# The first two projection steps in two halves of 256 tokens, with their weights and row tiles split over three engines

## The reference, cut to what matters

```python
x = x + layer(...)                     # SEQ 512 tokens, D_MODEL 1024, one layer
h = x * rsqrt(mean(x*x, -1) + 1e-6) * norm_g
proj = einsum('bsd,dc->bsc', h, w_in)  # 1024 -> 6656 columns
# dilated attention and block attention on parts of proj, gates, two branch
# projections, sigmoid merge, output projection, residual, final RMSNorm
```

## Time and profile before

| | |
|---|---|
| median of 3 runs | 429.91 us (429.64 to 429.94) |
| profiled execution, its own time | 429.92 us |
| its span, first to last instruction | 428.1 us |
| around the span | 1.8 us |
| PE busy | 417.7 us (98% of the span) |
| DVE, ACT, POOL busy | 302.8, 232.0, 220.9 us |
| mean granted PE clock | 0.996 |

### The profile page before, as it was taken

How to read it: one execution, slowest core, us unless ns; L and a number is a source line. 1 busy time by engine, 2 the same in 40 slices (tenths; PEclk the granted TensorE clock), 3 DMA queues, 4 the chain that set the end, 5 groups by cost and what they waited for, 6 DMA issues and landing times.

```text
span 428.1 us, 7122 instructions
## 1 busy us (share of the span) xinstructions
PE 417.7 (98%) x2526; PEld 372.5 (87%) x2526; DVE 302.8 (71%) x520; ACT 232.0 (54%) x487; POOL 220.9 (52%) x158
## 2 busy tenths in 40 slices
PE   7899999999999999999999999999999999999994
PEld 6789998889889988998888888889999999988884
DVE  3879946385856777657865773696686768589956
ACT  5745557554864764657656563454454545532634
POOL 5954533252655634574459655444335433734790
PEclk9999999999999999999999999999999999999998
DMA  8893454937899768222421335540443134199905
GB/s 272 250 262 102 152 163 143 280 132 260 278 303 388 290 213 273 100 100 54 144 99 50 100 127 205 196 136 14 122 138 108 48 116 136 38 410 393 418 7 198
DMA packets 49187, 77.23 MB, mean 180 GB/s; under 512 B 4440, under 2 KB 39296, under 8 KB 47616
## 3 DMA queue, kind: packets, MB, share of 16 engines
q1 hardware_dynamic: 44256, 67.91, 47.9%
q10 hardware_dynamic: 4896, 8.86, 5.7%
HBM read 55.73 MB, written 14.74 MB: 165 GB/s over the span
## 4 chain that ended last, share of the span: by engine, by line
PE 94%; DMA 2%; ACT 1%; DVE 1%; issue 1%; SPq 0%; DVEq 0%; ACTq 0%
PE ps L1183 15%; PE ps L1187 15%; PE ps L1184 15%; PE ps L1408 5%; PE ps L1407 5%; PE ps L1406 5%; PE ps L1224 4%; PE ps L1226 4%; PE ps L1225 4%; PE ps L1296 4%; PE ps L1277 3%; PE ps L1455 3%; PE ps L1453 3%; PE ps L1454 3%; PE ps L1315 2%; PE ps L1337 2%
## 5 line engine op out<-in xcount | busy, mean ns | idle before, releaser
L993 POOL TENSOR_TENSOR w_lo<-raw,w_hi 128x1024 fp32r<-128x1024 f32 x39 | 96.8, 2483 | 103.5 <-ACT w_hi L1507 103.5
L1183 PE MATMUL ps<-hT_hi,w_hi 128*128 128x512 f32 x240 | 95.7, 399 | 1.1 <-DVE hT_lo L1913 1.1
L1187 PE MATMUL ps<-hT_lo,w_hi 128*128 128x512 f32 x240 | 93.8, 391 | 0.0
L1184 PE MATMUL ps<-hT_hi,w_lo 128*128 128x512 f32 x240 | 93.6, 390 | 0.0
L1075 POOL TENSOR_TENSOR w_lo<-raw,w_hi 128x512 fp32r<-128x512 f32 (+1 forms) x34 | 42.5, 1270 | 49.5 <-ACT w_hi L1529 49.5
L1187 PEld LDWEIGHTS ps<-hT_lo,w_hi 128*128 128x128 f32 x240 | 45.0, 188 | 9.9
L1183 PEld LDWEIGHTS ps<-hT_hi,w_hi 128*128 128x128 f32 x240 | 45.1, 188 | 8.4 <-issue 1.3
L1184 PEld LDWEIGHTS ps<-hT_hi,w_lo 128*128 128x128 f32 x240 | 45.2, 188 | 7.0
L1224 PE MATMUL ps<-w_hi,hT_hi 128*128 128x256 f32 x160 | 45.2, 283 | 0.0
L1226 PE MATMUL ps<-w_lo,hT_hi 128*128 128x256 f32 x160 | 44.7, 279 | 0.0
L1225 PE MATMUL ps<-w_hi,hT_lo 128*128 128x256 f32 x160 | 44.6, 279 | 0.0
(11 more groups left out here) (279 smaller groups left out, 1048.0 us busy)
## 6 DMA issues: line engine op xcount, KB each, us to landing
raw<-in_w_in SPq DMA_DIRECT2D x25, 1024.0 KB, 5.6
KTs<-KTs SPq DMA_DIRECT2D x20, 256.0 KB, 4.4
folds<-folded_early SPq DMA_DIRECT2D x4, 1024.0 KB, 9.3
wq_raw<-in_w_out SPq DMA_DIRECT2D x4, 1024.0 KB, 9.7
folded<-folds SPq DMA_DIRECT2D x4, 1024.0 KB, 6.4
t_three<-output_weight_sums SPq DMA_DIRECT2D x2, 2048.0 KB, 11.5
output_weight_sums<-ws_parts ACTq DMA_DIRECT2D x6, 512.0 KB, 6.1
raw<-in_w_out SPq DMA_DIRECT2D x3, 1024.0 KB, 5.0
```

The lines of the kernel that those rows point to most:

```text
L993: nc.gpsimd.tensor_tensor(ring(w_lo, n, kt), src, ring(w_hi, n, kt).bitcast(F32), ALU.subtract).then_inc(lo_ready, 1)
L1183: pe.matmul(out, wh, hh, start=(k == 0), stop=False)
L1184: pe.matmul(out, wl, hh, start=False, stop=False)
L1187: return pe.matmul(out, wh, hl, start=False, stop=(k == kts - 1))
```

## The change

It cuts the opening into two halves of 256 tokens (row tiles 0 and 1, then 2 and 3).

- SP issues tiles 0 and 1, then the first chunk in two halves by k (k 0 to 3, k 4 to 7; all 256 columns each), then tiles 2 and 3.
- PE turns tiles 0 and 1, then runs matmuls of 256 tokens for steps 0 and 1 side by side, k by k, lows one k behind the highs. Just ahead of k = 7 it turns tiles 2 and 3 (`turn_rows`). Then follow k = 7, the last lows, and the second 256 tokens, step 0 and then step 1.
- Every tile is scaled half by ACT (high half, `scale_high_half`) and half by DVE (low half). Tile 0 is squared on ACT alone; of tiles 1, 2 and 3 ACT squares the low and DVE the high half (`square_high_half`), and `variance` adds two sums.
- The first chunk's cast and lows are made in four pieces of two k-tiles and all 256 columns: POOL does it all but the cast of piece 2, which ACT makes (`first_weights`). `lows(1)` is gone.
- The turned halves lie in banks 2 to 7 (first) and in banks 2, 3, 6, 7 (second), two k-tiles to a bank where needed. The gains are turned into bank 1, `gb_ready` comes in two steps.
- `d_hex` is made at step 10 (`spread_apart`).

The diff, cut to its core:

```diff
+PAIR_BANKS = [[2, 3, 4, 5, 6, 7, 4, 5], [2, 3, 6, 7, 2, 3, 6, 7]]
+TURN_ORDER = [[0, 1, 2, 3, 6, 7, 4, 5], list(range(8))]
+HI_TURNS = [[1, 2, 5, 6, 7, 8, 5, 6], [5, 6, 7, 8, 5, 6, 7, 8]]
+HIGH_SCALED = [1, 2, 4, 5]
 # SP
+            for i in range(2):
+                load_rows(i)
+            for e in range(2):
+                ks = slice(4 * e, 4 * e + 4)
+                sp.dma_start(first[:, ks, :], w_in_t[:, ks, at:at + 256]).then_inc(first_half_in[e], 16)
+            for i in range(2, TT):
+                load_rows(i)
 # POOL
+            for m in range(FIRST_PIECES - 1):
+                pool.wait_ge(first_half_in[m // 2], 16)
+                if m == ACT_PIECE:
+                    pool.wait_ge(opened_by_act, 3)
+                else:
+                    nc.gpsimd.tensor_copy(hi, part).then_inc(first_hi, 1)
+                    pool.wait_ge(first_hi, m + 1)
+                nc.gpsimd.tensor_tensor(lo, part, hi.bitcast(F32), ALU.subtract).then_inc(first_lo, 1)
...
 # PE
+            for i in range(2):
+                turn_rows(i)
+            for k in range(KT_D):
+                if k == KT_D - 1:
+                    for i in range(2, TT):
+                        turn_rows(i)
+                for n in range(2):
+                    first_high(n, 0, k)
+                if k:
+                    first_lows(k - 1)
+            first_lows(KT_D - 1)
+            for n in range(2):
+                for k in range(KT_D):
+                    first_high(n, 1, k)
+                    first_low_weights(n, 1, k)
+                    if k:
+                        first_low_rows(n, 1, k - 1)
+                first_low_rows(n, 1, KT_D - 1)
 # ACT
+            square_rows(0, D)
+            root(0)
+            square_rows(1, D // 2)
+            scale_high_half(0)
+            root(1)
+            scale_high_half(1)
+            turned_high(0, range(2))
+            first_weights()
+            turned_high(0, range(2, 4))
+            square_rows(2, D // 2)
+            turned_high(0, range(4, 6))
+            square_rows(3, D // 2)
+            root(2)
+            turned_high(0, range(6, KT_D))
+            scale_high_half(2)
+            root(3)
+            scale_high_half(3)
+            turned_high(1, range(KT_D))
 # DVE
+            variance(0)
+            square_high_half(1)
+            scale_low_half(0)
+            variance(1)
+            turn_gain()
+            scale_low_half(1)
+            turned_low(0, range(2))
+            halve_bias()
+            square_high_half(2)
+            turned_low(0, range(2, 4))
+            square_high_half(3)
+            variance(2)
+            turned_low(0, range(4, 6))
+            variance(3)
+            scale_low_half(2)
+            turned_low(0, range(6, KT_D))
+            scale_low_half(3)
+            turned_low(1, range(KT_D))
```

More of the change, by code:

```diff
@@ L1155, in _ @@
                 pe.matmul(ps[:, 0, 0:P], ident[:, :], ident[:, :], start=True, stop=True)
[L1157 to L1161, removed]
-                for k in range(KT_D):
[L1163 to L1172, removed]
+            pe.wait_ge(vec_in, 32)
@@ new lines, in _, with turn_rows @@
+            pe.transpose(ps[:, 1, 0:24], vecs[:, :], ident[0:24, 0:24]).then_inc(vecs_turned, 1)
+            def turn_rows(i):
+                order = TURN_ORDER[i // 2]
+                for k in order:
+                    if k == order[0]:
+                        pe.wait_ge(x_scaled, i + 1)
+                    if k == order[4]:
+                        pe.wait_ge(opened_by_act, HIGH_SCALED[i])
+                    if i == 2 and k in (0, 2):
+                        pe.wait_ge(hT_lo_ready, 6 if k else 2)
+                    last = pe.transpose(pair_place(i // 2, k)[:, P * (i % 2):P * (i % 2) + P],
+                                        xs[:, i, P * k:P * k + P], ident[:, :])
+                    if i % 2:
+                        last.then_inc(x_turned, 1)
@@ new lines, in first_high @@
+            def first_high(n, p, k):
+                if n == 0:
+                    pe.wait_ge(hT_hi_ready, KT_D * p + k + 1)
+                    if p == 0 and k // 2 == ACT_PIECE:
+                        pe.wait_ge(opened_by_act, 3)
+                    elif p == 0 and k < 6:
+                        pe.wait_ge(first_hi, k // 2 + 1)
+                    elif p == 0:
+                        pe.wait_ge(hi_ready, 2)
+                elif p == 0 and k == 0:
+                    pe.wait_ge(gb_ready, 1)
+                pe.matmul(ps[:, n, 256 * p:256 * p + 256], ring(w_hi, n, KT_D)[:, k, :], pair_of(hT_hi, p, k),
+                          start=(p == 0 and k == 0), stop=False)
@@ new lines, in first_low_weights, with first_low_rows @@
+            def first_low_weights(n, p, k):
+                if n == 0 and p == 0 and k < 6:
+                    pe.wait_ge(first_lo, k // 2 + 1)
+                elif n == 0 and p == 0:
+                    pe.wait_ge(lo_ready, 2)
+                pe.matmul(ps[:, n, 256 * p:256 * p + 256], ring(w_lo, n, KT_D)[:, k, :], pair_of(hT_hi, p, k),
+                          start=False, stop=False)
+            def first_low_rows(n, p, k):
+                if n == 0:
+                    pe.wait_ge(hT_lo_ready, KT_D * p + k + 1)
+                last = pe.matmul(ps[:, n, 256 * p:256 * p + 256], ring(w_hi, n, KT_D)[:, k, :],
+                                 pair_of(hT_lo, p, k), start=False, stop=(p == 1 and k == KT_D - 1))
+                if p == 1 and k == KT_D - 1:
+                    last.then_inc(projected, 1)
@@ L1204, in column_tile @@
                 def column_tile(k):
[L1205 to L1210, removed]
                     last = term(ps[:, pbank(n), :], k, KT_D, ring(w_hi, n, KT_D)[:, k, :],
-                                ring(w_lo, n, KT_D)[:, k, :], hT_hi[:, k, :], hT_lo[:, k, :],
-                                hh_count=k + 1 if n == 0 else 0)
+                                ring(w_lo, n, KT_D)[:, k, :], hT_hi[:, k, :], hT_lo[:, k, :])
                     if k == KT_D - 1:
@@ L1340, in values @@
                 last.then_inc(valued, 1)
-            for s in range(NS):
+            for s in range(2, NS):
                 score, turn = [], []
@@ L1607, in root, with scale_high_half @@
                 nc.scalar.activation(rstd[:, i:i + 1], rvar[:, i:i + 1], ACT.Sqrt).then_inc(rstd_ready, 1)
-            def scale_low_half(i):
+            def scale_high_half(i):
                 act.wait_ge(rstd_ready, i + 1)
[L1611 to L1617, removed]
+                half = xs[:, i, D // 2:D]
+                nc.scalar.activation(half, half, ACT.Copy, scale=rstd[:, i:i + 1]).then_inc(opened_by_act, 1)
@@ new lines, in variance, with turned_low @@
+                nc.vector.reciprocal(rvar[:, i:i + 1], var[:, i:i + 1]).then_inc(var_ready, 1)
+            def turned_low(p, ks):
+                for k in ks:
+                    dve.wait_ge(hT_hi_ready, KT_D * p + k + 1)
+                    nc.vector.scalar_tensor_tensor(out=pair_of(hT_lo, p, k), in0=pair_place(p, k),
+                                                   scalar=gb[:, k:k + 1], in1=pair_of(hT_hi, p, k).bitcast(F32),
+                                                   op0=ALU.mult, op1=ALU.subtract).then_inc(hT_lo_ready, 1)
@@ L1886, in turn_vectors, with turn_gain, halve_bias @@
+            def turn_gain():
                 dve.wait_ge(vecs_turned, 1)
-                link(nc.vector.tensor_copy(gb[:], ps[:, 7, SEQ - 24:SEQ]))
+                nc.vector.tensor_copy(gb[:], ps[:, 1, 0:24]).then_inc(gb_ready, 1)
+            def halve_bias():
+                dve.wait_ge(gb_ready, 1)
                 nc.vector.tensor_scalar(hbias[:], gb[:, 8:24], 0.5, None, ALU.mult).then_inc(gb_ready, 1)
-            for i in range(HALVED):
-                variance(i)
-                scale_rows(i, 0)
@@ L1893, in _ @@
[L1893 to L1913, removed]
-                                               in1=hT_hi[:, k, :].bitcast(F32), op0=ALU.mult,
-                                               op1=ALU.subtract).then_inc(hT_lo_ready, 1)
+            variance(0)
```

134 lines of the change are left out of this document (73 added, 61 removed).

## The result

| | before | after |
|---|---|---|
| median (17 runs each) | 429.76 us (429.42 to 430.86) | 430.37 us (430.15 to 431.8) |
| profiled execution, its own time; span | 429.92; 428.1 us | 430.72; 428.9 us |
| step 2 begins | 25.17 | 25.93 |

The ratio of the times is 1.0016 [1.0009, 1.0023]. The change costs 0.6 us: the ratio is inside the 0.2% that counts here as no change, though its interval lies above 1 and reaches 0.23%. The forecast was 431.4 (429.2 to 432.2).

The account below looks back on a forecast made before the run. PE, busy from 14.20 us, passes the opening on whole. Tile 3 scaled at 18.69 plus 7.93 puts step 2 at 26.62 against 25.17; 429.92 + 1.45 = 431.4 us, range 429.2 to 432.2.

Parts of the forecast that it names:

- Bound and passing on: PE is busy throughout from 14.20 us, so any change in the opening passes on whole; step 2 1.45 us later.
- What PE has left at S: After tile 3 is scaled (S), PE needs 7.93 us to step 2: a wait, eight transposes and 58 matmuls.
- The price of the cut: Steps 0 and 1 as 96 narrow instead of 48 wide matmuls: 11.52 against 10.97, 0.55 us.
- The port: In the opening, DVE and POOL block each other for whole instructions at SBUF; by this rule the time is 431.4 us.
- The sign that I had asked for: DVE's squares and variances of tiles 2 and 3 last 1 us and more, each ending as a POOL instruction ends.
- rival 1: No port waits in the opening, DVE's own list decides: step 2 at 24.57, 429.3 us, or 428.9 with earlier loads; 20%.
- Rival 2: Small DVE instructions, the variance sums, pass the port: 431.1 us, or 430.3 in a second form; 20%, half each.
- second form: Tile 2 lands before 11.1, its square precedes lows 1, variance 2 runs at once: S 17.57, 430.3 us; half of 20%.
- the sum's clock on POOL: Instruction-by-instruction times of POOL and DVE in the opening: lows 1 at 11.1, lows 3 until 16.77, tile 3 scaled at 18.69.
- They hardly meet before the change: Before the change POOL has no weights until 11.29; DVE's last SBUF-only opening instruction ends at 11.71, so they hardly meet.
- Loads: Chunk halves land at about 8.1 and 9.7, tiles 2 and 3 at 11.3 and 12.9, each 3.2 us later.
- rivals 3 and 4: Step 2's weights late, up to 431.9 us, 8%; PE clock falls between 14 and 18.7, 432.6 to 438 us, 7%.

Follow-up runs that it names:

- e2: The changed kernel with tiles 2 and 3 squared whole on ACT and root(3) ahead of both high halves; 429.23 us, ratio 0.9985 to the kernel before.
- e5: The kernel before, with only the matmuls of steps 0 and 1 cut into two of 256 tokens; step 2 at 25.54 us, no whole time given.
- e3: The changed kernel with POOL's four subtractions for the first chunk's lows replaced by memsets of zero, which read nothing; 428.71 us.
- f5: The changed kernel with POOL making the lows of piece 2 twice; 430.14 us.
- i2: The changed kernel itself, with no edit, profiled once more; 430.17 us.
- i1: The changed kernel with POOL's lows of piece 1 held until DVE has squared its half of tile 2; 430.74 us.
- e1: The changed kernel with the two-input sum of variance written as a tensor_scalar taking the second sum as a scalar operand; 429.96 us.
- g1: The kernel before, with only the three d_hex instructions moved to step 10; 429.17 us.
- f3: The changed kernel with only POOL's last lows of the first chunk held until tile 3 is scaled; 430.49 us.
- e4: The changed kernel with tiles 2 and 3 loaded ahead of the first chunk's second half; 431.61 us.

## Why the prediction was right or wrong

**Bound and passing on: right.** Step 2 came 0.76 later and the span grew by 0.8.

**What PE has left at S: right.** 7.94 in seven executions (e2's too), forecast 7.93. The price of the cut, 0.61 by e5, was given as 0.55.

**The port: right in mechanism and place.** Squares of 1.79 and 0.85, a last cast of 1.07, variances that wait, each ending with or shortly behind an instruction of the other engine. The sign that I had asked for, all four on DVE with 1 us and more, held for one of them only (1.79; the others 0.85, 0.44 and 0.54), but the sum itself had waits of 1.0, 0.36, 0.49 and 0.31 on them, so that sign was set too high. e3 puts its price at 1.94 us from A to S. This is also the answer to where the gain went: without these waits the same order gives 428.71, that is rival 1's 428.9 to 429.3 and a little better. The Trainium skill, SBUF — State Buffer, Who interferes with whom, says that whoever issues first gets the shared pair for the whole instruction. The trace agrees where the starts are 0.1 us and more apart; f5 and i2 against after show how much this hangs on 0.1 us. Closer than that the start in the row does not tell who is first: in after the scaling of tile 1 began at 8.07 and still waited (0.91) for POOL's cast of 8.09, which took its bare 0.61.

**Rival 2 falls.** Sums of 128x1 with two SBUF inputs took 0.44 and 0.54, up to 1.12 in f5 and i1, against 0.16 free. By e1 and the table this costs some 0.38; I had charged 0.30. Of its second form (the square slips in ahead of the lows and variance 2 runs at once, S 17.57) f5 shows the first half only: there variance 2 took 1.12, and POOL had more to do. That its S of 17.42 is near 17.57 is chance.

**The wrong step: the sum's clock on POOL.** I had S at 18.69, 0.70 late. The term "lows 1 11.1 to 12.35" began at 10.74, 0.36 sooner: I had let lows 0 wait for the whole scaling of tile 1, to 9.2, and it began at 8.78 and took 1.33, 0.06 over its 1.27. So lows 0 did not wait for the end of the scaling in the row (8.98). From the start of lows 1 to the end of lows 3 were 5.47 instead of 5.67, and from there to S 1.78 instead of 1.92: the chain lost less at each change of hands than the full recorded durations that I had summed. An instruction that was held ends sooner behind the one that held it than its free duration: a sum (free 0.16) ended 0.02 behind POOL's instruction (16.23 against 16.21), a scaling (free 0.47) 0.29 behind it in e2 (16.13 against 15.84). So the mechanism stood and a size was off; it was enough to bring the time from what I gave 60% (slower by over 0.2%) to what I gave 28%. The rest of the miss, 0.35 from the profiled execution's 430.72 to the median of 430.37, is less than the 0.55 between after and i2, and the prediction had no term for this spread. What did not hold is the call itself, slower by over 0.2%.

**"They hardly meet before the change": only half right.** In the trace I read, two scalings of halves took 0.86. In g1 and e5, where the opening is that of before, the same pair took longer, as the chunk landed sooner. Their DVE rows, g1 and then e5:

```profile
10.20 1.22 DVE L1877 TENSOR_SCALAR xs<-xs,rstd 128x512 f32<-128x512 f32 x2
```
```profile
10.49 2.25 DVE L1890 TENSOR_SCALAR xs<-xs,rstd 128x512 f32<-128x512 f32 x2
```

In e5 this was worth 1.4 on DVE. So of the three executions read here with the opening of before, the port held DVE's scalings in two, and it held DVE in both of the changed kernel's.

**Loads, rivals 3 and 4.** In after tile 2 was issued at 2.65 and landed 8.1 later, tile 3 at 3.3 and 8.8 later: at 10.75 and 12.1, not 11.3 and 12.9 (in i2 at 10.05 and 11.4). Tile 3's load was never waited for. Tile 2's was, in e1 and f3 (0.66 and 0.70), and in after it landed only 0.09 ahead of A, so it lies close to the path. The second half was fed, `hT_hi` in 3.03 for eight. Step 2's weights did not end last: their lows ended at 25.30. The granted clock stayed at 1.00 with gaps up to 0.53. The moved gains' transpose stood behind PE's opening matmuls until 7.70 and let DVE start tile 1's scaling only at 8.07; I had costed that place at nothing, and what it cost alone was not tried. In e1 and f3 the scaling of tile 1 began at 7.43 and 7.24, and A was still 10.53 and 10.78, since DVE then waited for tile 2; there its place had no part in A.

## What to carry to other kernels

Before work is added to POOL under a list of DVE instructions that read SBUF twice, write both lists side by side and mark every pair that both need the port; count the waits, not the busy time, and look above all at what each engine asks for within 0.1 us of the other. The cure was to take the two-input work to ACT (429.23) and, with it, to let POOL's last piece wait for the scaling that the critical path needs (428.72); holding the piece alone gave nothing (430.49). An opening whose order is settled by such races needs several executions before a difference of half a microsecond is read.

## What the runs showed of the hardware that I had not expected

- The form of a small DVE instruction decides whether it waits for POOL: a 128x1 sum of two SBUF tiles took up to 1.12, the same sum with one of them as a scalar operand 0.20 under POOL's lows, while a 128x16 `tensor_scalar` took 1.17 against 0.17.
- A table instruction of POOL waits too: the 128x128 affine select at 5.49 took 0.85 in after, beside DVE's square of tile 1 that began at 5.52, and 0.29 in i2, where that square began at 5.67. In e1, with starts of 5.47 and 5.51, it was the square that waited (0.80) and the select took 0.29.
- PE's half clock came within 2.36 us of idling in e4 (the granted clock was 1.00 until 12.6 and 0.50 from 12.8) and lasted until about 16, with pairs of 256-token matmuls 0.43 apart instead of 0.24; gaps of 1.40 brought none.
